# Weight slots at byte 128 of a 1,024-byte line in place of byte 64, and the last activation tile at the common pitch

## The reference

```python
proj = rms_norm(x) @ w_in                                   # 2048 -> 6448
x = x + concat(rwkv7_mixer(proj), gdn_mixer(proj)) @ w_out  # 2048 -> 2048
h = rms_norm(x)
x = x + (silu(h @ ffn_w_gate) * (h @ ffn_w_up)) @ ffn_w_down      # 2048 -> 5632 -> 2048
x = rms_norm(x)
x = x + fox_mixer(rms_norm(x), fox_w_in, ...) @ fox_w_out   # 2048 -> 6160, 2048 -> 2048
x = x + conv_ffn(rms_norm(x), ffn_w_up_2, ffn_w_down_2)     # 2048 -> 11264, 5632 -> 2048
```

## Time and profile before

| | |
|---|---|
| median of three runs | 2491.35 us |
| the profiled execution | 2490.99 us, span 2489.3 us |
| TensorE busy | 2437.2 us, 98% of the span |
| VectorE, ScalarE, GpSimd busy | 59%, 45%, 5% |
| share of TensorE in the chain that ended last | 92% |
| the three matmul lines' share in that chain | 29%, 29%, 28% |
| DMA | 173 GB/s mean |
| stretch of the recurrences | 298.4 to 544.8 us |
| stretch of attention between its products | 1633.2 to 1669.9 us |

### The profile page before, as it was taken

How to read it: one execution, slowest core, us unless ns; L and a number is a source line. 1 busy time by engine, 2 the same in 40 slices (tenths; PEclk the granted TensorE clock), 3 DMA queues, 4 the chain that set the end, 5 groups by cost and what they waited for, 6 DMA issues and landing times.

```text
span 2489.3 us, 57370 instructions
## 1 busy us (share of the span) xinstructions
PE 2437.2 (98%) x24650; PEld 2409.3 (97%) x24650; DVE 1477.2 (59%) x1686; ACT 1123.4 (45%) x1064; POOL 114.8 (5%) x93
## 2 busy tenths in 40 slices
PE   8999989989999999999999999999999999999999
PEld 8999978889999999999999999989999999999998
DVE  5557588664654545554444567674576666765444
ACT  5333524444544444443344544363555555544332
POOL 3000050000200000000020100000200000000000
PEclk9999989999999999999999999999999999999999
DMA  7555300126555555556565565625555555555554
GB/s 233 187 193 195 119 2 4 37 86 188 197 191 192 196 186 197 190 191 196 188 198 191 188 239 200 221 83 188 187 199 189 191 197 186 197 190 190 197 190 150
DMA packets 171387, 431.72 MB, mean 173 GB/s; under 512 B 17614, under 2 KB 23387, under 8 KB 170107
## 3 DMA queue, kind: packets, MB, share of 16 engines
q1 hardware_dynamic: 170027, 422.30, 50.3%
q10 hardware_dynamic: 1232, 7.52, 0.8%
HBM read 427.59 MB, written 2.17 MB: 173 GB/s over the span
## 4 chain that ended last, share of the span: by engine, by line
PE 92%; DVE 6%; ACT 1%; POOL 1%; issue 0%; DMA 0%; DVEq 0%; SPq 0%; ACTq 0%; POOLq 0%
PE ps L1970 29%; PE ps L1971 29%; PE ps L1972 28%; PE ps L2124 1%; POOL SQ L528 1%; DVE TM L1366 0%; DVE LO L1370 0%; DVE TT L1367 0%; DVE CV L1400 0%; ACT HIW L606 0%; DVE LOW L1083 0%; DVE GT L1382 0%; PE ps L2162 0%; DVE TMP L1313 0%; PE ps L2068 0%
## 5 line engine op out<-in xcount | busy, mean ns | idle before, releaser
L1083 DVE TENSOR_TENSOR LOW<-RAW,HIW 128x2048 fp32r<-128x2048 f32 (+1 forms) x396 | 910.3, 2299 | 915.4 <-ACT HIW L606 915.4
L1970 PE MATMUL ps<-H_ROWS,HIW 128*128 128x256 f32 x4928 | 1366.7, 277 | 4.5 <-DVE H_ROWS L1122 1.3
L1971 PE MATMUL ps<-H_ROWS,HIW 128*128 128x256 f32 x4928 | 1365.6, 277 | 0.0
L1972 PE MATMUL ps<-H_ROWS,LOW 128*128 128x256 f32 x4928 | 1364.5, 277 | 0.0
L606 ACT ACTIVATE HIW<-RAW 128x2048 fp32r<-128x2048 f32 (+1 forms) x396 | 759.4, 1918 | 1180.1 <-PE ps L1972 1170.4
L1970 PEld LDWEIGHTS ps<-H_ROWS,HIW 128*128 128x128 f32 x4928 | 927.1, 188 | 6.2 <-issue 4.6
L1972 PEld LDWEIGHTS ps<-H_ROWS,LOW 128*128 128x128 f32 x4928 | 927.8, 188 | 0.0
L1971 PEld LDWEIGHTS ps<-H_ROWS,HIW 128*128 128x128 f32 x4928 | 926.5, 188 | 0.1
L1970 PE MATMUL ps<-HID,HIW 128*128 (+1 forms) x1408 | 388.7, 276 | 0.0
L1971 PE MATMUL ps<-HID,HIW 128*128 (+1 forms) x1408 | 388.6, 276 | 0.0
L1972 PE MATMUL ps<-HID,LOW 128*128 (+1 forms) x1408 | 388.6, 276 | 0.0
(11 more groups left out here) (367 smaller groups left out, 1514.1 us busy)
## 6 DMA issues: line engine op xcount, KB each, us to landing
RAW<-in_ffn_w_up SPq DMA_DIRECT2D x264, 512.0 KB, 4.3
RAW<-in_ffn_w_down SPq DMA_DIRECT2D x176, 512.0 KB, 4.8
RAW<-in_fox_w_in SPq DMA_DIRECT2D x98, 512.0 KB, 4.4
RAW<-in_w_in SPq DMA_DIRECT2D x96, 512.0 KB, 4.1
RAW<-in_ffn_w_gate SPq DMA_DIRECT2D x88, 512.0 KB, 3.6
RAW<-in_w_out SPq DMA_DIRECT2D x32, 512.0 KB, 5.0
RAW<-in_fox_w_out SPq DMA_DIRECT2D x32, 512.0 KB, 4.6
INV<-rows_out ACTq DMA_DIRECT2D x4, 1024.0 KB, 7.3
```

The lines of the kernel that those rows point to most:

```text
L1083: V.tensor_tensor(LOW[:, u_const % 4, 0:n], RAW[:, u_const % 4, 0:n], HIW[:, u_const % 2, 0:n].bitcast(F32), ALU.subtract).then_inc(lo_mad ...
L1970: mm(o_, hi_w, h_hi, start=start, stop=False)
L1971: mm(o_, hi_w, h_lo, start=False, stop=False)
L1972: i = mm(o_, lo_w, h_hi, start=False, stop=stop)
```

## The change

Two numbers move the weight slots and what is laid over them from byte 64 to byte 128 modulo 1,024, and a third puts LAST to 0, so that tile 15 of H starts at 256 and 768 as the other tiles do. No instruction is added, removed or moved on any engine.

```diff
-LAST = 60
+LAST = 0
...
-        w0 = o + 64
+        w0 = o + 128
         RAW = at("RAW", [P, RAW_SLOTS, UNIT], w0)
         LOW = at("LOW", [P, RAW_SLOTS, UNIT], w0, F32R); o += 32768
-        HIW = at("HIW", [P, HI_SLOTS, UNIT], o + 64, F32R); o += 16384
+        HIW = at("HIW", [P, HI_SLOTS, UNIT], o + 128, F32R); o += 16384
         o += 256
```

## The result

The changed kernel takes 2590.47 us (median of 4 runs, 2585.03 to 2592.51) against 2491.37 us: a ratio of 1.0394, 95% interval [1.038, 1.0407]. It is 3.9% slower, where 2491 us was forecast and the range ended at 2520.

What follows compares the result with a forecast made beforehand. TensorE, busy 98%, was taken as the bound: 19,008 large matmuls times the distance between their starts. Profiled 2490.99 us, less 5.5 for tile 15, plus 5.5 for longer slow stretches, plus 0, gave 2491 us; range 2479 to 2520.

Steps and rivals of the forecast that it cites:

- Tile 15 at the common pitch: Gate-up groups: the last tile's matmuls no longer run at 119.2 ns, saving 5.5 us over 38 groups.
- the shake that goes: `w_out` and attention's output: tile 15 no longer ends slow stretches, so 13 more units run slow, twice: +5.5 us.
- The sums of squares: Feed-forward net's first group, between fifth and sixth unit: their waits restore the fast pace; otherwise 17.6 us per net.
- The short matmuls: Attention's input: they may leave the slow pace behind in up to 4 groups; bounds 0 and 6.7 us, taken as 0.
- Weight slots at 128: All large matmuls: weights' relation to moving data goes from 192 to 128 bytes modulo 512; taken as no cost.
- The upper bound: Moved weight slots: at worst all large matmuls run at the slow pace, +4.4 ns each.
- rival C: Every unit of the large products: the slow pace is the only one with weights at 128; 2565 us, chance 0.18.
- C's counter-argument: Against an only-slow kernel: tile 15 differs by 48 bytes modulo 64, the new relation by a whole 64.
- The other engines at nothing: ScalarE and VectorE: the moved addresses cost nothing; rounding and subtraction would be hidden behind TensorE too.
- Both signs: Forecast wrong if any steady pace but 113.3 and 117.8 ns appears, or recurrences' 246.4 us change by over 1 us.
- Rival A: Large products: the slow pace disappears with weights at 128, saving 9.6 us in all; 2481 us, chance 0.28.

Runs made afterwards that it cites:

- the best one: Against the changed kernel, all tiles of H and HID start 240 bytes later, weights still at byte 128: 2484.42 us, ratio 0.9972 to the kernel before.

## Why the prediction was wrong

*Tile 15 at the common pitch, 5.5 us, and the shake that goes, 5.5 us back.* As a pair right in size: with LAST alone the ratio is 0.9996. That is luck in part, for one step of it was wrong. The sums of squares do not reliably restore the fast pace: in the profiled run they left it slow, and all 148 units from the attention's output to the end ran slow. The forecast counted 13 units in every run; the ten runs spread over 36 us, and no trace shows how many slow units the ones near the median had.

*The short matmuls*, taken at nothing: right where it could be seen. In the profiled run with LAST alone, the attention's groups 2 to 6 stayed fast.

*Weight slots at 128: "I take nothing, because the fast and the slow pace both occur at one relation, so the relation alone does not set the pace now."* This is the step that failed. The rows showed that history chooses among the paces that one distance offers. They said nothing on which paces another distance offers, and I took the first for the second. The term, put at nothing, is +101 us in the profiled runs: not one unit kept 113.3 ns. With LAST at 60 it is 3.4%.

*The upper bound, 4.4 ns a matmul, and rival C (2565 us, 0.18).* C had the place right, every unit from the first on, and its sign came true (down products listed above 276 ns). Its pace was wrong: 117.8 ns, which it wanted everywhere, occurs nowhere in the changed kernel. I bounded an unmeasured pace by the slowest steady pace seen, though tile 15, at 119.2 ns, already showed a higher one. It would have given 19,008 x 5.9 = 112 us over an all-fast kernel and 2593 us. That the kernel landed just under it is luck, a mixture of two other paces; but a range that ended there would have held it.

*C's counter-argument*, that a whole 64 bytes would matter less than 48, fell too: a step of 64 bytes, from distance 192 to 128 or 256, costs 5.3 to 6.7 ns against the fast pace.

*The other engines at nothing* held: same durations per instruction. Both signs by which the forecast was to be known as wrong came. The first, a steady pace other than 113.3 and 117.8 ns, is the failure. The second, recurrences that change by more than 1 us, was set too narrow: they took 1.5 us more, and from kernel to kernel they differ by up to 5 (below). Rival A, no slow pace with weights at 128, did not come; a kernel without it was found only once the moving tiles had moved too.

The Trainium skill, "SBUF — State Buffer", section "Who interferes with whom", gives TensorE two independent read ports and says that it waits for no one. If that were the whole story the time would not have changed. The fourteen pairs of starts in the table, with paces from 113.3 to 120.0 ns for the same matmuls, contradict it for this kernel. Whether the reads of weights and moving data collide in the memory or on the way to the array, no run here shows. That both starts count, with neither alone deciding, is shown.

## What to carry to other kernels

Where TensorE is busy for the whole span, read the distance between starts, in nanoseconds, for each stretch. A pace 6% slower (120.0 for 113.3 ns) showed in the listed duration as 283 to 285 for 276 ns, and in TensorE's busy share not at all, 98% before and after. If one form has two steady paces, the start addresses of stationary and moving operand are a parameter to sweep together, over 256 bytes in steps of at most 64 and at a few finer places, and look for a pair that has the fast pace only; a pair with a single pace can also be the slowest, as distance 256 is here. A bound for an untried setting comes at least from the worst stretch seen, however short. Even that is no ceiling: tile 15 showed 119.2 ns, and 120.0 came, with kernels of up to 2605 us.

## What the runs showed of the hardware that was not expected

- Steady paces of one and the same matmul (256 columns, 128x128 weights) from 113.3 to 120.0 ns, with repeating patterns: in the kernel with all tiles shifted and weights at 64, nine matmuls repeat (117, 123, 120, 117, 123, 117, 117, 120, 119 ns).
- No steady pace was faster than 113.3 ns, under any pair of starts.
- The recurrences took 246.4, 247.9 and 251.3 us for the same work, with a granted clock of 0.97, 0.96 and 0.95. Of the seventeen profiled kernels eleven took 246.3 to 246.6 us, five 247.9 to 248.4 and only the best one 251.3. Each kernel was profiled once, so whether its layout or the single run makes the difference is not shown. The rows are of the kernel with LAST alone, the changed kernel and the best one: stretch, length, busy us (count) of TensorE, its weight loads, VectorE, ScalarE and GpSimd, then granted clock, DMA share and GB/s.

```profile
297.10:543.50 246.40, 213.69 (x5259) 195.02 (x5257) 189.31 (x336) 107.25 (x247) 34.97 (x19) 0.97 0.10 33
```
```profile
308.60:556.50 247.90, 216.28 (x5259) 197.09 (x5257) 188.93 (x336) 107.25 (x247) 34.98 (x19) 0.96 0.10 33
```
```profile
296.50:547.80 251.30, 221.09 (x5263) 201.07 (x5261) 188.40 (x336) 107.50 (x247) 35.06 (x19) 0.95 0.10 32
```
